# Output projections with both column halves of row tiles 0 to 3 first, and a row affine in two fused instructions

## The reference

```python
def first_block(x, ...):
    ...
    u = _layer_norm(x) * (1.0 + scale1) + shift1
    m = _token_mixer(u, ...)                                    # ... mixed @ w_out
    x = _layer_norm(DEEPNORM_ALPHA * x + gate1 * m, ln1_w, ln1_b)
    u2 = _layer_norm(x) * (1.0 + scale2) + shift2
    f = jnp.square(jax.nn.relu(u2 @ w_ff1)) @ w_ff2
    x = _layer_norm(DEEPNORM_ALPHA * x + gate2 * f, ln2_w, ln2_b)

def second_block(x, ...):
    ...
    y = concatenate([y_ssd, y_s5, y_rg]) @ w_out
    h = layer_norm(ALPHA * h + y, ln1_g, ln1_b)
    h = layer_norm(ALPHA * h + cross_attention(h, mem, ...), ln2_g, ln2_b)
    h = layer_norm(ALPHA * h + squared_relu_mlp(h, mlp_w1, mlp_w2), ln3_g, ln3_b)
```

## Time and profile before

| | |
|---|---|
| median of 3 runs | 3345.58 us (3342.49 to 3348.52) |
| the profiled execution | 3346.45 us |
| its span, first to last instruction | 3344.7 us |
| mean granted TensorE clock | 0.896 |
| busy: TensorE, VectorE, ScalarE, GpSimd | 81%, 48%, 32%, 26% |
| first projection, first job to hidden job 4 | 696.5 to 860.4 us |
| second projection, first job to TensorE's next work after the columns | 2260.5 to 2368.5 us |
| third projection, first job to hidden job 4 | 2543.8 to 2667.8 us |

### The profile page before, as it was taken

How to read it: one execution, slowest core, us unless ns; L and a number is a source line. 1 busy time by engine, 2 the same in 40 slices (tenths; PEclk the granted TensorE clock), 3 DMA queues, 4 the chain that set the end, 5 groups by cost and what they waited for, 6 DMA issues and landing times.

```text
span 3344.7 us, 34229 instructions
## 1 busy us (share of the span) xinstructions
PE 2702.0 (81%) x13254; PEld 1397.4 (42%) x13254; DVE 1593.5 (48%) x2203; ACT 1074.0 (32%) x1287; POOL 879.8 (26%) x282
## 2 busy tenths in 40 slices
PE   2789758786899999997877882338589799999997
PEld 1467545543344444443453431114344344444443
DVE  5544453247344444465355479974423632222225
ACT  2332322212522222224423254314433532222221
POOL 0543350010111111124221026531600431111114
PEclk9899867888899999998888996668799899999998
DMA  6222220020111111120121120001101011111111
GB/s 237 76 64 76 67 76 26 26 88 1 51 51 50 50 50 50 51 63 14 51 82 41 55 76 0 0 0 63 51 19 45 26 51 51 50 50 50 50 38 51
DMA packets 95598, 172.84 MB, mean 52 GB/s; under 512 B 5601, under 2 KB 37745, under 8 KB 94705
## 3 DMA queue, kind: packets, MB, share of 16 engines
q1 hardware_dynamic: 81072, 130.50, 12.0%
q10 hardware_dynamic: 14400, 40.65, 3.4%
HBM read 164.85 MB, written 6.29 MB: 51 GB/s over the span
## 4 chain that ended last, share of the span: by engine, by line
PE 64%; DVE 15%; ACT 6%; issue 5%; DVEq 5%; POOLq 1%; PEld 1%; DMA 1%; ACTq 1%; POOL 0%; PEldq 0%; SPq 0%
PE PS L592 19%; PE PS L593 19%; PE PS L594 19%; DVE XT L1878 1%; ACT S L1305 1%; ACT WS L1344 1%; ACT WB L1343 1%; PE PS L1269 1%; ACT XT L1310 1%; DMA R<-in_x 1%; DVE S L2536 1%; DVEq L2538 1%; PE PS L1242 1%; DVE S L2530 1%; DVE ST L1897 1%
## 5 line engine op out<-in xcount | busy, mean ns | idle before, releaser
L459 POOL TENSOR_TENSOR WB<-WS,WB 128x2048 f16<-128x2048 f32 x108 | 448.7, 4176 | 1978.4 <-ACT WS L1344 1978.2
L592 PE MATMUL PS<-XT,WB 128*128 128x512 f16 (+1 forms) x1584 | 609.1, 385 | 85.9 <-DVE Hf L1868 25.7
L593 PE MATMUL PS<-XT,WB 128*128 128x512 f16 (+1 forms) x1584 | 608.4, 384 | 0.0
L594 PE MATMUL PS<-XT,WB 128*128 128x512 f16 (+1 forms) x1584 | 607.6, 384 | 0.0
L592 PE MATMUL PS<-WB,Hf 128*128 128x512 f16 x1440 | 551.1, 383 | 30.5 <-DVEq L1881 10.0
L593 PE MATMUL PS<-WB,Hf 128*128 128x512 f16 x1440 | 550.7, 382 | 0.0
L594 PE MATMUL PS<-WB,Hf 128*128 128x512 f16 x1440 | 550.2, 382 | 0.0
L1343 ACT ACTIVATE WB<-WS 128x2048 f16<-128x2048 f32 (+3 forms) x118 | 212.5, 1801 | 585.2 <-PEq L601 552.6
L1868 DVE CAST Hf<-S 128x512 f16<-128x512 f32 x128 | 108.3, 846 | 447.2 <-ACT S L1556 447.2
L592 PEld LDWEIGHTS PS<-XT,WB 128*128 128x128 f16 (+1 forms) x1584 | 156.5, 99 | 286.2 <-issue 54.6
L2175 DVE SCALAR_TENSOR_TENSOR R<-PS,R 128x512 f32<-128x512 f32 x176 | 120.9, 691 | 264.5 <-PE PS L594 260.7
(11 more groups left out here) (350 smaller groups left out, 3502.1 us busy)
## 6 DMA issues: line engine op xcount, KB each, us to landing
WS<-in_w_ff SPq DMA_DIRECT2D x32, 1024.0 KB, 5.1
WS<-in_mlp_w SPq DMA_DIRECT2D x32, 1024.0 KB, 5.1
Hf<-in_w_ada ACTq DMA_DIRECT2D x16, 1024.0 KB, 7.6
WS<-in_w_in SPq DMA_DIRECT2D x48, 256.0 KB, 4.2
Hf<-in_w_ada SPq DMA_DIRECT2D x8, 1024.0 KB, 10.5
WS<-in_w_out SPq DMA_DIRECT2D x8, 1024.0 KB, 5.1
WS<-in_w_in SPq DMA_DIRECT2D x14, 512.0 KB, 3.8
R<-in_x SPq DMA_DIRECT2D x1, 4096.0 KB, 14.6
```

Source lines behind the costliest of these rows:

```text
L459: pool.tensor_tensor(WB[:, slot, 1, hf * 2048:(hf + 1) * 2048], WS[:, hf, :], WB[:, slot, 0, hf * 2048:(hf + 1) * 2048], ALU.subtract).the ...
L592: pe.matmul(o, ah, bh, start=(first and k == 0), stop=False, skip_group_check=True)
L593: pe.matmul(o, ah, bl, start=False, stop=False, skip_group_check=True)
L594: mm = pe.matmul(o, al, bh, start=False, stop=(last and k == n - 1), skip_group_check=True)
```

## The change

It edits four things. In all three projections TensorE does the column half 0 of tiles 0 to 3, then half 1 of tiles 0 to 3, then half 0 of tiles 4 to 7 and half 1 of tiles 4 to 7; so the first chunk is used up four jobs later. VectorE follows with its own order: adds of half 0 for tiles 0 to 3, then for each tile the add of half 1 and its norm, with the half-0 adds of tiles 4 and 5 behind tile 2 and those of tiles 6 and 7 behind tile 3. `norm_tail` rounds the first chunk behind tile 3's normalise instead of ahead of all tiles, except after the first MLP (`early=True`). The first layer's row affine becomes two scalar_tensor_tensor instructions: (R - mean) * row, then * reciprocal root + row. The variance is no longer copied into SD before the small constant is added to it, in all per-tile norms.

```diff
+        OUT_ORDER = [(n, t) for first in (0, 4) for n in range(2) for t in range(first, first + 4)]
...
             def out_projection(c0, A, src, ks=range(KT), started=False):
-                for n in range(2):
-                    pe.wait_ge(w_split, c0 + n + 1)
+                for n, t in OUT_ORDER:
+                    if t in (0, 4):
+                        pe.wait_ge(w_split, c0 + n + 1)
                     W = wide(c0 + n)
...
+                    if t == 7:
+                        chunk_used()
+                    if (n, t) == (1, 5):
+                        pe.wait_ge(rows_ready, rr[0] + 4)
+                        transpose_half(0, src)
                 second_half(src)
...
-            def norm_tail(roots, scale, bias, first):
-
-                round_chunk(first)
+            def norm_tail(roots, scale, bias, first, early=False):
+
+                if early:
+                    round_chunk(first)
                 for t in range(TT):
                     for _ in range(roots):
                         root_at(t)
                     normalise(S[:, 2 + t % 4, :] if roots == 2 else R[:, t, :], t)
                     if t == 3:
+                        if not early:
+                            round_chunk(first)
                         columns_half(0, scale, bias)
...
             def inv_root(n, eps, at=None):
                 c = slice(0, n) if at is None else slice(at, at + 1)
-                dve.tensor_scalar(SD[:, 0, c], SD[:, 0, c], eps, None, ALU.add).then_inc(var_ready, 1)
+                var = SD[:, 0, c] if at is None else MV[:, at, 1:2]
+                dve.tensor_scalar(SD[:, 0, c], var, eps, None, ALU.add).then_inc(var_ready, 1)
...
                 stats(R[:, t, :], t, D)
                 dve.drain()
-                dve.tensor_copy(SD[:, 0, t:t + 1], MV[:, t, 1:2])
-                dve.drain()
                 inv_root(1, eps, at=t)
                 if plain:
                     return hand_over(t)
-                dve.tensor_scalar(R[:, t, :], R[:, t, :], MV[:, t, 0:1], SD[:, 2, t:t + 1], ALU.subtract, ALU.mult)
-                dve.drain()
-                dve.tensor_tensor(R[:, t, :], R[:, t, :], S[:, 0, :], ALU.mult)
-                dve.drain()
-                return dve.tensor_tensor(R[:, t, :], R[:, t, :], S[:, 1, :], ALU.add)
+                dve.scalar_tensor_tensor(R[:, t, :], R[:, t, :], MV[:, t, 0:1], S[:, 0, :], ALU.subtract, ALU.mult)
+                dve.drain()
+                return dve.scalar_tensor_tensor(R[:, t, :], R[:, t, :], SD[:, 2, t:t + 1], S[:, 1, :], ALU.mult,
+                                                ALU.add)
+
+            def wide_job(at, n, t):
+                j = at + OUT_ORDER.index((n, t))
+                dve.wait_ge(job_done, j + 1)
+                return j % 4
...
+            late_adds = {2: (4, 5), 3: (6, 7)}
+            at = J[0]
+            for t in range(4):
+                dve.drain()
+                gated_add(wide_job(at, 0, t), t, 0, 9, True, M_SCALE)
+            dve.wait_ge(par_in["ln1"], 32)
+            scale_rows()
+            for t in range(TT):
+                dve.drain()
+                gated_add(wide_job(at, 1, t), t, 1, 9, True, M_SCALE)
+                dve.drain()
+                norm_twice(t)
+                for u in late_adds.get(t, ()):
                     dve.drain()
...
+                    gated_add(wide_job(at, 0, u), u, 0, 9, True, M_SCALE)
+                if t == 3:
+                    columns_half(0, XT)
             columns_half(1, XT)
+            J[0] += 2 * TT
```

More of the change, by code:

```diff
@@ L890, in out_projection @@
             def out_projection(c0, A, src, ks=range(KT), started=False):
-                for n in range(2):
-                    pe.wait_ge(w_split, c0 + n + 1)
+                for n, t in OUT_ORDER:
+                    if t in (0, 4):
+                        pe.wait_ge(w_split, c0 + n + 1)
                     W = wide(c0 + n)
[L896 to L906, removed]
+                    if started and n == 0 and t < 4:
+                        gemm(PS[:, J[0] % 4, :], lambda k: hilo(A, 6 + k, t * P, (t + 1) * P),
+                             lambda k: hilo(W, 6 + k, 0, HALF), 2, first=False).then_inc(job_done, 1)
+                        J[0] += 1
+                    else:
+                        rows_gemm(A, ks, t, (0, HALF), W)
+                    if t == 7:
[3 more added lines that the diff above has]
+                        transpose_half(0, src)
                 second_half(src)
@@ L1587, in mlp @@
                 else:
-                    norm_tail(1, lambda k: col("ln2_w", k), lambda k: col("ln2_b", k), C["z"])
+                    norm_tail(1, lambda k: col("ln2_w", k), lambda k: col("ln2_b", k), C["z"], early=True)
             K[0] = SIDE["mlp1"]
@@ L2199, in _ @@
             dve.wait_ge(x_in, 32)
-            for n in range(2):
-                if n == 1:
-                    dve.wait_ge(par_in["ln1"], 32)
-                    scale_rows()
-                for t in range(TT):
-                    dve.drain()
-                    b = wide_in()
-                    gated_add(b, t, n, 9, True, M_SCALE)
-                    if n == 1:
-                        dve.drain()
-                        norm_twice(t)
-                        if t == 3:
-                            columns_half(0, XT)
+            late_adds = {2: (4, 5), 3: (6, 7)}
[11 more added lines that the diff above has]
+                for u in late_adds.get(t, ()):
+                    dve.drain()
+                    gated_add(wide_job(at, 0, u), u, 0, 9, True, M_SCALE)
+                if t == 3:
+                    columns_half(0, XT)
             columns_half(1, XT)
+            J[0] += 2 * TT
             def mlp(gate, par, last):
@@ L2563, in out_rows @@
                     dve.wait_ge(res_ready, 16)
-                for n in range(2):
-                    if n == 1:
-                        dve.wait_ge(par_in[par], 32)
-                        scale_rows().then_inc(ln_rows, 1)
-                    for t in range(TT):
-                        dve.drain()
-                        b = wide_in()
-                        gated_add(b, t, n, None, False, scale)
-                        if n == 1:
-                            dve.drain()
-                            norm_rows(t, EPS)
-                            if t == 3:
-                                columns_half(0, XT)
+                at = J[0]
+                for t in range(4):
+                    dve.drain()
+                    gated_add(wide_job(at, 0, t), t, 0, None, False, scale)
+                dve.wait_ge(par_in[par], 32)
+                scale_rows().then_inc(ln_rows, 1)
+                for t in range(TT):
+                    dve.drain()
+                    gated_add(wide_job(at, 1, t), t, 1, None, False, scale)
+                    dve.drain()
+                    norm_rows(t, EPS)
+                    for u in late_adds.get(t, ()):
+                        dve.drain()
+                        gated_add(wide_job(at, 0, u), u, 0, None, False, scale)
+                    if t == 3:
+                        columns_half(0, XT)
                 columns_half(1, XT)
+                J[0] += 2 * TT
             K[0] = SIDE["o2"]
```

## The result

| | before | changed |
|---|---|---|
| time, median of 4 runs each (range) | 3345.65 us (3342.49 to 3348.52) | 3298.78 us (3297.98 to 3303.78) |
| ratio, 95% interval | | 0.9863 (0.9846 to 0.9880) |
| profiled execution, its span | 3346.45, 3344.7 us | 3297.98, 3296.2 us |

The account below looks back on a forecast made before the run. The first projection was taken as bound by how early VectorE starts its eight norms and how long each takes. Terms 24.6 + 8.5 + 0.9 + 1.6 + 0.2 = 35.8 us off 3345.6 gave 3309.8, range 3302 to 3321.

Parts of the forecast that it names:

- Part 1, the tile's norm: First layer's norms: without copies and with the fused affine, a tile costs 9.19 us instead of 10.43.
- the half rate: First layer's fused affine: a skill rule says scalar_tensor_tensor with two non-bf16 SBUF sources runs at half throughput; tile 11.8 us.
- rival B: First layer: fused instructions at half rate, 2.57 us each, so 15.0 us gained in all, 3330.6 us; chance 5%.
- Part 2, the order in the first layer: First projection: norms start 21.1 us earlier, rounding follows tile 3's normalise, columns follow rounding; 24.6 us gained.
- a sign of being wrong: Forecast is wrong if tiles stay at 10.4, transposes start over 2 us after 765, or columns wait on something besides rounding.
- Part 3: Second projection: tile 4 comes 7.7 us earlier, four remaining copies give 0.9; sum 8.5 us.
- Part 4: Third projection: TensorE bounds it, the head start is worth nothing, four copies give 0.9 us; bounds 0 and 0.9.
- Part 5, the last tail: Last MLP's tail: a copy is cover, not path, and only the first tile's counts; 0.2 us.
- Part 5, the first MLP's tail: First MLP's tail: VectorE's chain with seven copies on it, 1.6 us; bound 0.7 if TensorE's jobs end last.
- E: More than the sum: denser work keeps TensorE's clock up or stalls behind GpSimd fall away; 5 us more, 3305; chance 9%.
- A: Terms pass on only in part: bank wait, table load, query jobs, locked stretches; 29.5 us gained, 3316 us; chance 17%.
- C: Slower: rounding ahead of the columns costs 7.2 us per projection and the head start does not pay; +8.1, 3354; chance 3%.

Follow-up runs that it names:

- experiment 8: Changed kernel with the 7.2 us rounding put into ScalarE's gaps at tile 4 in the first and second projection: 3319.72 us, ratio 0.9926.
- experiment 4: Kernel before with only the one-column variance copies removed: 3333.43 us, ratio 0.9965.
- experiment 5: Changed kernel with the one-column copy put back in the last MLP's tail alone: 3304.02 us, ratio 0.9883.
- experiment 3: Kernel before with only the row affine fused into two scalar_tensor_tensor instructions: 3330.75 us, ratio 0.9965.
- The second pair: Changed kernel, unedited, measured again against the kernel before: 3305.72 us against 3341.80 us, ratio 0.9892.
- experiment 7: Changed kernel with GpSimd's residual released after the column pieces in the first MLP's tail and second projection: 3281.09 us, ratio 0.9816.
- experiment 11: Changed kernel with GpSimd's residual released after the columns in the third projection too, plus the one-source tiny instruction: 3270.80 us, ratio 0.9785.
- the best version: Changed kernel with the residual late in all three places and the tiny instruction as a tensor_scalar: 3270.80 us, ratio 0.9785.

## Why the prediction was wrong

- **Part 1, the tile's norm**: right. 9.24 against 9.19, the fused pair 1.28 each. The loss of 1.8 a tile that it gives for the half rate leaves the copies out; with them a tile of 11.8 against 10.43 would lose 1.3, as rival B reckons.
- **Part 2, the order in the first layer**: the size is right, 24.5 against 24.6, the transposes and the columns at their distances. One of its reasons is not: it takes the columns to wait for the rounding, and a wait for something else as a sign of being wrong. Experiment 8 shows that wait. The rounding lies beside TensorE's last jobs and costs nothing in the first projection; without it the columns start at the same time and wait for the transposes. Rounding and first transposes end together, so the sum came out right all the same, and that is luck. The prediction's own figures had the two within 0.6 to 1.6 us of each other (transposes at 765 to 766, columns at 766.6), so the 7.2 us that I expected of experiment 8 were never there.
- **Part 3**: right in mechanism, 9.2 against 8.5. Tile 4 came 7.8 earlier (predicted 7.7), the rest gave 1.4 in place of 0.9 (the two terms make 8.6).
- **Part 4**: 1.1 against 0.9, its upper bound. The reason given, four copies less, is not borne out: the copies alone made this stretch 1.3 longer (experiment 4). TensorE works without a gap over the last 30 us ahead of its last transposes here too, while the norms are done 11 to 12 us before. The size is luck.
- **Part 5, the last tail**: this is the step that failed. "In this loop a copy is cover, not path" was true of five tiles. But a wait behind another engine's instruction is a step function of the start. At tile 6, 0.2 us decided between 2.25 and 0.16; I read the 1.98 of one tile and not the 2.25 of the next, whose margin was 0.10. Tile 6 gives 2.1 of the gain, the shorter wait that follows at tile 7 (1.96 to 0.81) 1.2, and copies the rest. Predicted 0.2, measured 4.0 (experiments 4 and 5 show it from both sides).
- **Part 5, the first MLP's tail**: 3.2 against 1.6, and this step failed too. It took the tail for VectorE's chain with seven copies on it. TensorE's jobs end last, 11 us behind the last norm (experiment 4), which was the case of its lower bound, 0.7. What the copies add can be told from the stretch behind piece 120 alone: 0.7. The rest is 1.5 at a higher granted clock, whose cause stays open, and 0.9 from another meeting of column pieces and GpSimd.
- **The rivals**: E was the nearest, and I gave it 9% and 5 us; lined up, it was 6.2. Its stalls behind GpSimd did fall away. The clock was higher in one tail, but that denser work kept it up is not shown. A had 17%, and none of its margins broke. B is excluded by experiment 3. C fell.
- **The range**: I took the runs of before, 6 us apart, for noise around a median. They carry an early stretch that varies by 8 us from execution to execution, and the first profile of before was the latest of all thirteen at piece 28 (682.6 to 690.8). About 5 of the 46.9 us are that. Without them 3345.6 less 42.0 is 3303.6, inside the range of 3302 to 3321: the terms were 6.2 short, and the early stretch carried the median past the range's end. The second pair, 36.1 apart, would have looked like the forecast's 35.8, by the same chance.

## What to carry to other kernels

Line two traces up at instructions that both have, and compare stretches. Here that repeated to 0.2 and 0.4 us where medians of a few runs gave gains 11 us apart. Where an instruction waits for the end of another engine's, read its margin at every repetition, not its duration at one: a removed 0.2 us is worth nothing or the whole instruction. Where the sum of a stretch comes out, take its reasons away one by one all the same: the rounding and four copies of the third projection stood in it and were not on the path. And look first for what runs beside the column splitting: moving GpSimd's residual behind it gave about 30 us (20.3 in experiment 7, 9.4 more in experiment 11), against 42 of this change, for a moved increment of a semaphore at three places.

## What the runs showed of the hardware

- The one-column scalar_tensor_tensor with two SBUF sources waits for a running GpSimd tensor_tensor (up to 2.26 us for 0.16 of work); a tensor_scalar of the same size (0.21) and a reciprocal (0.16) do not. It is not a matter of two sources alone: in the best version VectorE's cast of 128x512, one SBUF source, fp32 to fp16, also takes 2.57 beside the residual, against 0.43 alone.
- A program that is the same reached the same point 8 us apart in two executions, and then ran 2650 us to within 0.2.
